# The mean square of x as two rounded products of a split sum, placed behind the second block row of slab 3

## What is computed

```python
def rms_norm(x, g):
    y = x * rsqrt(mean(x * x, axis=-1) + 1e-6)
    return y * g

h = rms_norm(x, g_mix)
qa, ka, va, qb, kb, vb, ga, gb = split(h @ w_in)
qa, ka, qb, kb = (rms_norm(per head) of each)
ya = moba_attention(qa, ka, va); yb = swa_attention(qb, kb, vb, sinks)
x = x + (sigmoid(ga) * (ya @ w_branch_a) + sigmoid(gb) * (yb @ w_branch_b)) @ w_out
x = x + square(relu(rms_norm(x, g_ffn) @ w_ff1)) @ w_ff2
```

## Time and profile before

| | |
|---|---|
| three runs | 679.95 us median (679.71 to 680.64) |
| profiled execution, its own time | 680.22 us |
| its span, first to last instruction | 678.3 us |
| PE busy | 672.8 us (99%) |
| DVE, ACT, POOL busy | 500.3, 369.1, 326.7 us |
| granted TensorE clock over the span | 1.000, the level of 2.4 GHz |

### The profile page before, as it was taken

One profiled execution on the slowest core, in us unless ns is written; L12 is line 12 of the kernel. 1 busy time (PEld: TensorE's weight loads), 2 busy tenths in 40 slices (PEclk: granted clock), 3 DMA queues, 4 the chain that ended last, 5 costly groups with the idle time before them and its releaser, 6 DMA issues.

```text
span 678.3 us, 9489 instructions
## 1 busy us (share of the span) xinstructions
PE 672.8 (99%) x3254; PEld 554.7 (82%) x3254; DVE 500.3 (74%) x691; ACT 369.1 (54%) x660; POOL 326.7 (48%) x195
## 2 busy tenths in 40 slices
PE   8999999999999999999999999999999999999998
PEld 6788788888888888888888888888888888888886
DVE  6875798455545554885468878788797878978897
ACT  7764676566655666543338536254463525536360
POOL 0466466555555443544337435346362454435532
PEclk9999999999999999999999999999999999999999
DMA  8223152222322213445222222414233151220303
GB/s 311 101 65 122 36 155 94 73 70 82 109 78 65 89 63 105 148 151 217 93 95 93 94 98 76 166 62 138 78 97 120 62 186 62 93 96 29 125 1 124
DMA packets 22908, 69.86 MB, mean 103 GB/s; under 512 B 2731, under 2 KB 4267, under 8 KB 22876
## 3 DMA queue, kind: packets, MB, share of 16 engines
q1 hardware_dynamic: 22588, 68.92, 30.3%
q10 hardware_dynamic: 288, 0.52, 0.2%
HBM read 67.27 MB, written 2.16 MB: 102 GB/s over the span
## 4 chain that ended last, share of the span: by engine, by line
PE 97%; DMA 1%; SPq 1%; DVE 0%; ACT 0%; issue 0%
PE bank L1268 22%; PE bank L1270 22%; PE bank L1269 22%; PE bank L1561 8%; PE bank L1560 7%; PE bank L1558 7%; PE bank L1412 3%; PE bank L1399 2%; PE bank L1432 1%; PE bank L1434 1%; DMA w_raw<-slabs 1%; SPq L380 1%; PE bank L1530 1%; PE bank L1294 0%; PE bank L1295 0%; PE bank L1304 0%
## 5 line engine op out<-in xcount | busy, mean ns | idle before, releaser
L468 POOL TENSOR_TENSOR w_lo<-w_raw,w_hi 128x1024 fp32r<-128x1024 f32 x79 | 196.0, 2485 | 230.4 <-ACT w_hi L556 230.3
L1268 PE MATMUL bank<-x_hi,w_hi 128*128 128x512 f32 x328 | 132.6, 404 | 0.2 <-DVE w_lo L863 0.2
L1270 PE MATMUL bank<-x_hi,w_lo 128*128 128x512 f32 x328 | 128.2, 391 | 0.0
L1269 PE MATMUL bank<-x_lo,w_hi 128*128 128x512 f32 x328 | 127.8, 390 | 0.0
L1268 PE MATMUL bank<-qk_hi,w_hi 128*128 128x512 f32 x320 | 125.0, 391 | 0.0
L1270 PE MATMUL bank<-qk_hi,w_lo 128*128 128x512 f32 x320 | 124.6, 389 | 0.0
L1269 PE MATMUL bank<-qk_lo,w_hi 128*128 128x512 f32 x320 | 124.5, 389 | 0.0
L556 ACT ACTIVATE w_hi<-w_raw 128x1024 fp32r<-128x1024 f32 x80 | 83.8, 1056 | 57.8 <-PE bank L1270 57.8
L1151 DVE SCALAR_TENSOR_TENSOR store<-bank,softmax,store 128x512 f32<-128x512 f32 x101 | 72.0, 743 | 23.7 <-PE bank L1561 23.7
L1561 PE MATMUL bank<-v_parts,x_lo 128*128 128x512 f32 (+1 forms) x218 | 84.4, 387 | 0.0
L1558 PE MATMUL bank<-v_parts,x_hi 128*128 128x512 f32 (+1 forms) x218 | 84.4, 387 | 0.0
(11 more groups left out here) (149 smaller groups left out, 1170.2 us busy)
## 6 DMA issues: line engine op xcount, KB each, us to landing
w_raw<-slabs SPq DMA_DIRECT2D x80, 512.0 KB, 3.3
bias_m<-slabs SPq DMA_DIRECT2D x16, 512.0 KB, 3.5
qk_hi_again<-slabs SPq DMA_DIRECT2D x16, 512.0 KB, 4.6
store<-x_t SPq DMA_DIRECT2D x16, 256.0 KB, 4.0
bias_m<-tab_dram SPq DMA_DIRECT2D x8, 256.0 KB, 4.2
out<-store SPq DMA_DIRECT2D x7, 256.0 KB, 2.1
bias_m<-tab_dram SPq DMA_DIRECT2D x8, 128.0 KB, 3.4
w_raw<-slabs ACTq DMA_DIRECT2D x1, 384.0 KB, 4.0
```

What stands on the lines that cost most here:

```text
L468: pool.tensor_tensor(w_lo[:, g % WS, :], w_raw[:, g % RAW, :], w_hi[:, g % WS, :].bitcast(F32), ALU.subtract).then_inc(w_lo_ready, lots)
L1268: pe.matmul(out_, wh, xh, start=first, stop=False)
L1269: pe.matmul(out_, wh, xl, start=False, stop=False)
L1270: last = pe.matmul(out_, wl, xh, start=False, stop=end)
```

## The change

x_sum is no longer multiplied in full float32. DVE computes the last of the seven additions twice: once into `x_sum_hi` in the rounded type, in an instruction that stands ahead of it, and then as before. A further instruction subtracts: `x_sum_lo` is `x_sum` less `x_sum_hi`. PE multiplies both with a column of 1/1024, broadcast to 128x128, in two matmuls of the rounded type that add up in the same bank, and they stand behind the second block row of slab 3 instead of behind the last one of slab 2. The column is set by one more memset of 128x1 at DVE's start. AFTER is as it was. The two parts lie in columns of `pt_hi` that are free then.

```diff
--- before.py
+++ after.py
@@ -135,6 +135,8 @@
 
         xsq = [store[:, j, :] for j in (8, 9, 10, 11)]
         x_sum = store[:, 12, :]
+        x_sum_hi, x_sum_lo = pt_hi[:, 2, :], pt_hi[:, 3, :]
+        mean_ones = pt_lo[:, 1, P:P + 1]
         r_inv_sq = store[:, 11, :]
         r_root, r_root_sq = store[:, 6, :], store[:, 10, :]
 
@@ -206,6 +208,7 @@
         acc_read = sem("acc_read")
         x_hi_ready, x_lo_ready = sem("x_hi_ready"), sem("x_lo_ready")
         xsq_ready, xsum_ready = sem("xsq_ready"), sem("xsum_ready")
+        xsum_hi_ready, xsum_lo_ready = sem("xsum_hi_ready"), sem("xsum_lo_ready")
 
         first_arrived = [sem("first_arrived0"), sem("first_arrived1")]
         first_ready = sem("first_ready")
@@ -839,6 +842,7 @@
                 for b in range(2):
                     last = dve.memset(head_ones[HD * a:HD * (a + 1), HD * b:HD * (b + 1)].bitcast(F32),
                                       1.0 / HD if a == b else 0.0)
+            dve.memset(mean_ones.bitcast(F32), 1.0 / D)
             last.then_inc(const_ready, 1)
             dve.memset(tabw[NBUCKET:NBUCKET + 1, :], MASK).then_inc(const_ready, 1)
             dve.wait_ge(par_arrived, 16)
@@ -879,7 +883,12 @@
                 dve.wait_ge(xsq_ready, k + 1)
                 if k > 1:
                     dve.wait_ge(xsum_ready, k - 1)
+                if k == KT - 1:
+                    dve.tensor_tensor(x_sum_hi, x_sum, xsq[k % 4], ALU.add).then_inc(xsum_hi_ready, 1)
                 dve.tensor_tensor(x_sum, x_sum, xsq[k % 4], ALU.add).then_inc(xsum_ready, 1)
+            dve.wait_ge(xsum_hi_ready, 1)
+            dve.wait_ge(xsum_ready, KT - 1)
+            dve.tensor_tensor(x_sum_lo, x_sum, x_sum_hi.bitcast(F32), ALU.subtract).then_inc(xsum_lo_ready, 1)
 
             def refine(out_, root_, square, x, ready, count):
 
@@ -1328,10 +1337,13 @@
                     pe.wait_ge(v_lo_ready, v_count(8))
                 pe.matmul(bank[5][0:NH, :], tabw, hot[:, S * h:S * h + S], start=True, stop=True).then_inc(tab_done, 1)
 
-            def mean_square(total, out_):
-
-                return pe.matmul(out_[:, :], ones[:, :].to_broadcast([P, P]), total, start=True, stop=True)
-
+            def mean_square(out_):
+
+                mean = mean_ones.to_broadcast([P, P])
+                pe.wait_ge(xsum_hi_ready, 1)
+                pe.matmul(out_[:, :], mean, x_sum_hi, start=True, stop=False)
+                pe.wait_ge(xsum_lo_ready, 1)
+                pe.matmul(out_[:, :], mean, x_sum_lo, start=False, stop=True).then_inc(ms_done, 1)
 
             pe.wait_ge(const_ready, 1)
             for _ in range(WARM_UP):
@@ -1373,9 +1385,8 @@
                         else:
                             pe.wait_ge(rest_ready, 2)
                     last = slab_part(g, acc(g), from_x, [kt], kt == 0, kt == KT - 1)
-                    if (g, kt) == (2, KT - 1):
-                        pe.wait_ge(xsum_ready, KT - 1)
-                        mean_square(x_sum, bank[5]).then_inc(ms_done, 1)
+                    if (g, kt) == (3, 1):
+                        mean_square(bank[5])
                     if (g, kt) in AFTER:
                         if AFTER[g, kt] == N_QKV - 2:
```

## The result

| | before | with the change |
|---|---|---|
| median of 22 runs each | 680.50 us (679.44 to 682.52) | 681.64 us (680.79 to 685.04) |
| ratio | | 1.0022 (95% interval 1.0014 to 1.0029) |
| profiled execution, time and span | 680.22, 678.3 us | 681.87, 680.0 us |

A forecast was written before the change was run, and what follows sets the result against it. PE, 99% busy, was taken as the bound, without slack at slab 7 against the ACT, DVE and POOL chain. Slab 7 3.5 late: 680.22 + 3.5 = 683.7, less 0.27 to the median, 683.4; range 681.5 to 684.3.

The forecast's parts named there:

- The sign: Whole kernel: the change makes it slower, above 681.3 us, given a chance of 0.89.
- the mechanism: Slab 3: added DVE instructions delay the splits of squares, PE waits, and the epsilon and ACT's first ln come late.
- the chain: From the mean square through ACT, DVE and POOL to slab 7, where PE has no slack; lateness 3.5 us passes on.
- the likeliest case: POOL's low part of slab 4 goes ahead of DVE's first split, which ends at 28.60; slab 7 3.5 late, 683.4, chance 0.52.
- the near tie: POOL's low part of slab 4 at 25.63 against DVE's first split at 25.66, 0.03 us apart; POOL taken first.
- no meeting: Rival: POOL's low part of slab 4 touches neither split; slab 7 1.26 us late, 681.2, chance 0.07.
- DVE first: Rival: first split precedes POOL's low part of slab 4, second ends at 29.15; slab 7 2.1 late, 682.0, chance 0.28.
- PE directly: PE's mean square: 1.11 us gone, two rounded products at 0.23 each added, a gain of 0.65 us taken alone.
- DVE: DVE's list at the squares' sum: subtraction starts at 25.06, first split at 25.66, ending no earlier than 26.35, before 24.94.
- The gain turned into a wait: PE, slab 3: reaches slab 0's head sum at 24.93 and waits at least 1.5 us for the first split.
- POOL, the step that failed: POOL's low part of slab 4 starts at 25.63, goes first, and holds the first split until 28.60.
- The three chances of being slower: POOL ahead of the split 0.52, DVE ahead 0.28, and a worse case of 684.5 us and more 0.10.

The follow-up runs named there:

- psum_early: Change, but the last square goes to a PSUM bank that both last additions read, and the products stand behind slab 2's last block row; 680.11 us.
- warm_hi_only: Change without the low part of the sum, one rounded product, 16 warm-up products instead of 10: 679.76 us; spelled without warm, it has 10: 680.12 us.
- round_alone: Change, but both rounded products stand behind the last block row of slab 2, where the old product stood; 681.91 us, ratio 1.0018.
- cold_after: The kernel with the change, with 2 warm-up products on PE instead of 10; 682.51 us.
- warm_after: The kernel with the change, with 16 warm-up products on PE instead of 10; 681.69 us.
- warm_pool_waits: Change, but POOL's low part of slab 4 waits for both splits of squares, 16 warm-up products: 681.45 us; spelled without warm, it has 10: 681.24 us.
- warm_before: The kernel before the change, with 16 warm-up products on PE instead of 10; 679.77 us.
- the move alone: Kernel before, with its full-precision product moved behind the second block row of slab 3, nothing added on DVE; 680.47 us, ratio 1.0006.

## Why the prediction was right, and where it was off

The sign, the mechanism and the chain were right; the likeliest case was the wrong one of the two that the near tie separates: it had been priced at 3.5 us at slab 7, where 2.05 came.

That the number lay in the range is partly luck. The median of 681.64 is 1.8 below the 683.4 that I gave and 0.14 above the range's lower end. I had reckoned from 679.95 for the kernel before, which came out at 680.50 in these 22 runs; with 679.95 the same ratio would give 681.4, just outside. The cost was forecast at 3.45 us and measured at 1.1 to 1.5. By the time alone "no meeting" (681.2) would fit as well as "DVE first" (682.0); it is the profile that decides.

- **PE directly.** Two products in turns of 0.23, as taken: 27.24, 27.46, 27.69.
- **DVE.** Subtraction at 10.44 from the first addition, first split at 11.06 (predicted 25.06 and 25.66 less 14.60, so 10.46 and 11.06), first split 0.68 long. Right to 0.02 us.
- **The gain turned into a wait.** Right: 1.4 us of wait ahead of the head sum of slab 0, where at least 1.5 was given; PE had come a little later against DVE in this execution.
- **POOL, the step that failed.** I let POOL's low part, at 25.63, come 0.03 ahead of the split, at 25.66. In the profiled execution POOL came at 11.09 from the first addition instead of 11.03, so 0.03 behind the split. The price of "DVE first" was 2.1 us at slab 7, the profile has 2.05; of the parts of that rival, the second split "ends at 29.15" came at 28.71 + 0.44 = 29.15, the epsilon at 28.63 + 0.44 = 29.07 for 29.07, ln at 29.78 for 29.80. The rule of the Trainium skill, "SBUF — State Buffer", "Who interferes with whom", that whoever issues first has the shared ports for the whole instruction, holds in the rows above (0.68 for the split that went first, 2.91 for POOL behind it, 2.89 for the split that was issued behind POOL); what it could not tell was who would be first.
- **The near tie can be read more finely than I did.** By the stamps of the trace in nanoseconds the sixth addition started 0 to 4 ns behind POOL's low part of slab 3 in eight executions, and DVE went first in all of them; in two it started 6 and 7 ns behind it, and POOL went first (psum_early, warm_hi_only). By that, POOL 30 ns ahead of the split, as I had it from before's phase, would have won; no run shows that case. My error was to take one execution's phase between POOL and DVE for fixed. In the profiled executions with the change's own list on DVE and no wait added on POOL (change, round_alone, cold_after, warm_after) POOL's low part of slab 4 came at 11.09, 11.34, 12.53 and 11.67, each time behind the first split. POOL held the first split only in psum_early, where the earlier tie had made the splits 0.23 later.
- **Two DVE instructions in a row.** The Trainium skill, "VectorE: DVE Perf Modes", section "The DRAIN you can't avoid", lets the next Vector instruction start only when the pipe is empty, but says that one that is not held starts earlier. The trace agrees with the second half: the second split, whose wait had long been met, started at 25.82, 0.61 behind a first one that took 0.68; the subtraction, which waits for the addition, started 0.78 behind one of 0.68. These are the 0.60 and 0.80 of the sum.
- **The other prices.** "No meeting" was priced at 1.26 us; with the meeting taken out, slab 7 came 1.31 behind before (warm_pool_waits against warm_before). The three chances of being slower add up to 0.90, where I wrote 0.89.
- **The chain.** ln late by 2.05, slab 7 by 2.05: no slack, as read from 49.81 and 49.87; shown by the constant 22.13 through all the kernels. This also holds for PE's own share: the move alone spared PE its wait and cost 0.34.
- **The size in time.** 1.1 to 1.5 us measured, 2.05 in the profiles. With 16 warm-up products, where PE's start varies less, the medians differ by 1.92. I read this so: part of the executions with 10 start with PE late, as the profiled ones of hi_only and pool_waits did, and then the change costs less, as in cold_after. The share of such executions was not measured, and no profile of the change with 10 shows it, so this stays an explanation and not a finding. The two slowest of the change, 684.55 and 685.04, would fit the tie going to POOL; neither was profiled.

## What to carry to other kernels

An engine that is busy 99% of the span can still have no slack against a chain of other engines, and then its own work is not what an edit should be priced by: look for the place where it starts within 0.06 us of what it waits for, and follow that chain back. Two instructions on an engine that is busy for only 74% of the span are not free if a shared port lies behind them; count what they push into whose turn. And before one execution's near tie is taken for an order, ask which waits at the program's start set the phase of the two engines, and look at a second profile.

## What the runs showed of the hardware

- POOL and a DVE instruction with two SBUF operands exclude each other: held splits and additions took 2.7 to 2.9 us in place of 0.69 (1.33 where the held one came late under POOL's), free ones with one operand in a bank of PSUM took 0.68 and 0.69 under the same POOL instruction.
- Which of the two goes first was decided within a few nanoseconds in ten near ties: 0 to 4 ns behind POOL by the stamps, DVE still won (8 of 8); 6 and 7 ns behind, it lost 2.25 us (2 of 2).
- With the same 10 warm-up products the upper clock level came at 4.1 us in one execution and at 10.4 in another. In pool_waits PE was back at matmuls 0.43 apart in slab 0, at a granted clock of 0.50 from 7.3 to 10.7 us, after a warm-up that had ended at the upper level and 1.5 us in which PE stood idle, up to 6.3 us.
